# A first stage in which dense products, modulation products and the split of the operands are put in another order

## The reference

```python
m_l = (jax.nn.silu(c) @ mod_w + mod_b)[:, None, :]
m_c = jax.nn.silu(c_ctx) @ mod_w + mod_b
sh1_l, sc1_l, g1_l, sh2_l, sc2_l, g2_l = jnp.split(m_l, 6, axis=-1)
sh1_c, sc1_c, g1_c, sh2_c, sc2_c, g2_c = jnp.split(m_c, 6, axis=-1)
p_lat = _ada(x, norm1, sh1_l, sc1_l) @ w_in      # _ada = rmsnorm(x, g) * (1 + scale) + shift
p_ctx = _ada(ctx, norm1, sh1_c, sc1_c) @ w_in
```

## Time and profile before

| what | value |
| --- | --- |
| median of three runs | 2082.76 us (2080.64 to 2083.97) |
| the profiled execution, its own time | 2093.51 us |
| its span in the trace | 2091.7 us |
| TensorE, VectorE, ScalarE, GpSimd busy | 91%, 57%, 40%, 13% of the span |
| mean granted TensorE clock | 0.955 |
| the first stage in the trace | 0 to about 201 us |

### The profile page before, as it was taken

One profiled execution on the slowest core, in us unless ns is written; L12 is line 12 of the kernel. 1 busy time (PEld: TensorE's weight loads), 2 busy tenths in 40 slices (PEclk: granted clock), 3 DMA queues, 4 the chain that ended last, 5 costly groups with the idle time before them and its releaser, 6 DMA issues. The chain is left out here.

```text
span 2091.7 us, 42194 instructions
## 1 busy us (share of the span) xinstructions
PE 1906.8 (91%) x18192; PEld 1663.0 (80%) x18192; DVE 1189.3 (57%) x2005; ACT 834.7 (40%) x1533; POOL 282.0 (13%) x341
## 2 busy tenths in 40 slices
PE   5999787878788999999999889999979999979997
PEld 4787445877767888888987779999769999769997
DVE  3322756446455752353466767855667756657753
ACT  3321464314223421122243645544454445454432
POOL 0200300502304000001300420111021002121001
PEclk8999986997999999999999999999989999999998
DMA  7621872002033323323231055555325546325543
GB/s 249 165 81 61 275 229 81 4 19 87 5 120 104 96 86 101 96 86 101 90 121 52 1 182 162 182 184 183 98 81 162 191 154 199 101 81 162 182 161 101
DMA packets 249003, 255.04 MB, mean 122 GB/s; under 512 B 6914, under 2 KB 247186, under 8 KB 248690
## 3 DMA queue, kind: packets, MB, share of 16 engines
q1 hardware_dynamic: 247344, 251.19, 37.3%
q0 software_dynamic: 864, 0.98, 0.4%
q10 hardware_dynamic: 610, 0.18, 0.0%
HBM read 251.28 MB, written 1.05 MB: 121 GB/s over the span
## 5 line engine op out<-in xcount | busy, mean ns | idle before, releaser
L529 DVE TENSOR_TENSOR RING_rounded<-RING,SC_rounded 128x1024 fp32r<-128x1024 f32 (+2 forms) x390 | 459.3, 1221 | 253.3 <-ACT SC_rounded L522 253.2
L549 PE MATMUL bank<-OT_rounded,SC_rounded 128*128 128x256 f32 (+1 forms) x1808 | 578.2, 320 | 25.2 <-DVE RING_rounded L529 8.5
L550 PE MATMUL bank<-HT_rounded,SC_rounded 128*128 128x256 f32 (+1 forms) x1808 | 573.5, 317 | 0.0
L551 PE MATMUL bank<-OT_rounded,RING_rounded 128*128 128x256 f32 (+1 forms) x1808 | 571.0, 316 | 0.0
L522 ACT ACTIVATE SC_rounded<-RING 128x1024 fp32r<-128x1024 f32 (+2 forms) x390 | 372.2, 1006 | 330.5 <-DMA RING<-in_l_mlp_w 187.3
L549 PEld LDWEIGHTS bank<-OT_rounded,SC_rounded 128*128 128x128 f32 x1808 | 344.7, 191 | 57.3 <-DVE RING_rounded L529 10.3
L551 PEld LDWEIGHTS bank<-OT_rounded,RING_rounded 128*128 128x128 f32 x1808 | 344.2, 190 | 26.1
L550 PEld LDWEIGHTS bank<-HT_rounded,SC_rounded 128*128 128x128 f32 x1808 | 344.6, 191 | 22.6
L549 PE MATMUL bank<-PT_rounded,SC_rounded 128*128 128x256 f32 (+1 forms) x896 | 277.9, 310 | 4.7 <-DVE RING_rounded L529 4.7
L550 PE MATMUL bank<-PT_rounded,SC_rounded 128*128 128x256 f32 (+1 forms) x896 | 276.9, 309 | 0.0
L551 PE MATMUL bank<-PT_rounded,RING_rounded 128*128 128x256 f32 (+1 forms) x896 | 276.0, 308 | 0.0
(11 more groups left out here) (546 smaller groups left out, 2742.0 us busy)
## 6 DMA issues: line engine op xcount, KB each, us to landing
RING<-in_l_mlp_w SPq DMA_DIRECT2D x64, 1024.0 KB, 5.3
RING<-in_w_ffn_in SPq DMA_DIRECT2D x44, 1024.0 KB, 5.1
RING<-in_l_mod_w SPq DMA_DIRECT2D x40, 1024.0 KB, 6.2
RING<-in_l_w_in SPq DMA_DIRECT2D x25, 1024.0 KB, 5.5
RING<-in_w_ffn_out SPq DMA_DIRECT2D x16, 768.0 KB, 4.6
RING<-in_w_in SPq DMA_DIRECT2D x10, 1024.0 KB, 5.4
RING<-in_w_ffn_out SPq DMA_DIRECT2D x16, 640.0 KB, 4.1
PT<-in_l_mod_w SPq DMA_DIRECT2D x8, 1024.0 KB, 9.7
```

What stands on the lines that cost most here:

```text
L529: net.nc.vector.tensor_tensor(low, whole, net.high4(s, m)[:, 0:self.w.kts[s], :].bitcast(F32), ALU.subtract).then_inc(self.split_ready, 1)
L549: net.nc.tensor.matmul(bank[:, tokens], high, x_high, start=start, stop=False)
L550: net.nc.tensor.matmul(bank[:, tokens], high, x_low, start=False, stop=False)
L551: return net.nc.tensor.matmul(bank[:, tokens], low, x_high, start=False, stop=stop)
```

## The change

The order of all three compute engines in the first stage is rewritten, and nothing else. Parameter rows: `c` and `c_ctx` are still fetched by ScalarE, the 13 other early ones by SyncE, between the first modulation slab and the second. Front: the last token block is transposed in `turn_order` and each bank is announced by itself; VectorE copies five banks, ScalarE three; the inverse roots are spread before `add(0)`; VectorE multiplies two tiles, does the first pair, and the other six tiles after it. Sums of the slabs go to two buffers in turn (`mod_rows`), so `copy(k)` waits for `fold(k-2)` only. `products` takes one half m at a time, and adds and folds of the next pair are put between the dense products of the pair at hand. ScalarE rounds the first half of a weight slab ahead of a pair's shift (slab 0) or between two copies (slabs 1, 2); VectorE's `operand(p)` is cut into `shift(p)` and `split(p)`.

```diff
...
+    mod_rows = [mod.rows, net.SC[:, 8968:9224]]
...
-    copy_order = [6, 7, 0, 1, 2, 3, 4, 5]
+    turn_order, copies_by_dve, copies_by_act = [7, 6, 0, 3, 1, 4, 2, 5], [7, 6, 0, 1, 2], [3, 4, 5]
...
+        places = [(g, sum(c for _, c in tile[:n]), name, count)
+                  for g, tile in enumerate(ROWS) for n, (name, count) in enumerate(tile)]
+        n_now = len(ROWS[0])
...
+                if k == 0:
+                    fetch_rows(sp, places[2:n_now])
...
-                    last = nc.tensor.matmul(sections[:, 2 * k + m, :], mod.rows[:, P * m:P * m + P],
+                    last = nc.tensor.matmul(sections[:, 2 * k + m, :], mod_rows[k % 2][:, P * m:P * m + P],
...
-                for f in range(KT):
+                for f in turn_order if t == NCH - 1 else range(KT):
...
-                last.then_inc(turned, 1)
-            pe.wait_ge(c_ready, 2)
+                    if t == NCH - 1:
+                        last.then_inc(turned, 1)
             pe.wait_ge(copied, 2)
-            add(0)
...
             last.then_inc(root_spread, 1)
+            add(0)
+            pe.wait_ge(rows_in[0], 16 * (len(ROWS[0]) - 2))
+            pe.wait_ge(copied_by_act, len(copies_by_act))
+            turn_rows(0, net.ps[5])
             add(1)
-            pe.wait_ge(rows_in[0], 16 * (len(ROWS[0]) - 2))
-            pe.wait_ge(copied, KT)
-            turn_rows(0, net.ps[5])
             pe.wait_ge(rstd_ready, 1)
             fold(0)
             fold(1)
-            products(0, (0, 1))
+            pe.wait_ge(copied, len(copies_by_dve))
+            products(0, 0, (0, 1))
             add(2)
+            products(0, 1, (0,))
+            add(3)
             fold(2)
-            add(3)
+            products(0, 1, (1,))
             fold(3)
+            products(1, 0, (0, 1))
+            products(1, 1, (0, 1))
+            products(0, 0, (2, 3))
+            products(0, 1, (2, 3))
+            add(4)
+            products(1, 0, (2, 3))
+            add(5)
+            fold(4)
+            products(1, 1, (2,))
+            fold(5)
+            products(1, 1, (3,))
             pe.wait_ge(cols_ready, 1)
-            products(0, (2, 3))
-            products(1, (0, 1))
-            add(4)
-            products(1, (2,))
-            fold(4)
-            add(5)
-            products(1, (3,))
-            fold(5)
-            products(0, (4, 5))
-            products(1, (4, 5))
-            products(2, (0, 1))
+            for kts in ((0, 1), (2, 3)):
+                for m in range(2):
+                    products(2, m, kts)
+            products(0, 0, (4, 5))
             add(6)
-            products(2, (2,))
+            products(0, 1, (4,))
+            add(7)
             fold(6)
-            add(7)
-            products(2, (3,))
+            products(0, 1, (5,))
             fold(7)
-            products(2, (4, 5))
+            for q in (1, 2):
+                for m in range(2):
+                    products(q, m, (4, 5))
             for q in range(by_pairs):
-                products(q, (6, 7))
+                for m in range(2):
+                    products(q, m, (6, 7))
...
-                if k:
-                    act.wait_ge(mod.folded, k)
-                act.activation(mod.rows, mod.sums, ACT.Copy).then_inc(mod.copied, 1)
+                if k > 1:
+                    act.wait_ge(mod.folded, k - 1)
+                act.activation(mod_rows[k % 2], mod.sums, ACT.Copy).then_inc(mod.copied, 1)
...
-            fetch_rows(places[:n_now])
+            fetch_rows(act, places[:2])
...
-            copy(0)
+            for f in copies_by_act:
+                act.wait_ge(turned, turn_order.index(f) + 1)
+                act.activation(net.XT[:, f, :], net.ps[f][:, :], ACT.Copy).then_inc(copied_by_act, 1)
...
+            copy(0)
             copy(1)
+            part.high(act, 0, 0)
             operand(0)
-            highs(0)
+            part.high(act, 0, 1)
             copy(2)
+            part.high(act, 1, 0)
             copy(3)
+            part.high(act, 1, 1)
             operand(1)
-            highs(1)
             copy(4)
+            part.high(act, 2, 0)
             copy(5)
+            part.high(act, 2, 1)
             operand(2)
-            highs(2)
             copy(6)
             copy(7)
             operand(3)
             highs(3)
-            fetch_rows(places[n_now:])
+            fetch_rows(act, places[n_now:])
...
-            def operand(p):
...
+
+            def split(p):
                 for t in (2 * p, 2 * p + 1):
                     dve.wait_ge(high_ready, t + 1)
                     nc.vector.tensor_tensor(HR[:, t, :], HT[:, t, :], OR[:, t, :].bitcast(F32),
                                             ALU.subtract).then_inc(split_ready, 1)
...
-            dve.wait_ge(turned, NCH)
-            for f in copy_order:
+            def norm(t):
...
+            for f in copies_by_dve:
+                dve.wait_ge(turned, turn_order.index(f) + 1)
                 nc.vector.tensor_copy(net.XT[:, f, :], net.ps[f][:, :]).then_inc(copied, 1)
+            dve.wait_ge(rstd_ready, 1)
+            norm(0)
+            norm(1)
             take_rows(0, net.ps[5])
             dve.wait_ge(cols_ready, 1)
-            dve.wait_ge(copied, KT)
-            dve.wait_ge(rstd_ready, 1)
-            for t in range(KT):
-                nc.vector.tensor_tensor(HT[:, t, :], net.XT[:, t, :], rstd, ALU.mult).then_inc(normed, 1)
-            operand(0)
-            lows(0)
-            operand(1)
+            shift(0)
+            part.low(dve, 0, 0)
+            split(0)
+            part.low(dve, 0, 1)
+            for t in range(2, KT):
+                norm(t)
             lows(1)
-            operand(2)
+            shift(1)
+            split(1)
             lows(2)
-            operand(3)
+            shift(2)
+            split(2)
+            shift(3)
+            split(3)
             lows(3)
```

More of the change, by code:

```diff
@@ L2160, in first_stage, with fetch_rows @@
         part = Part(net, st, "in0", w_in, Operand(OR, HR), banks=6)
+        places = [(g, sum(c for _, c in tile[:n]), name, count)
+                  for g, tile in enumerate(ROWS) for n, (name, count) in enumerate(tile)]
+        n_now = len(ROWS[0])
+        def fetch_rows(queue, some):
+            for g, r, name, count in some:
+                a = ins[name]
+                if len(a.shape) == 2:
+                    a = a.rearrange("a b -> (a b)")
+                into = rows[r:r + count, g, :]
+                queue.dma_start(into, a.rearrange("(t p) -> t p", p=P)).then_inc(
+                    c_in if g == 0 and r < 16 else rows_in[min(g, 1)], 16)
         @st.sync
@@ L2232, in turn_rows, with products @@
                 nc.tensor.transpose(bank[:, 0:r], rows[0:r, g, :], ident[0:r, 0:r]).then_inc(rows_turned, 1)
-            def products(q, kts):
-                for m in range(2):
-                    if kts[0] == 0:
-                        part.ready(pe, q, m)
-                    for kt in kts:
-                        pe.wait_ge(split_ready, kt + 1)
-                        step = part.passes(q, m, kt, everything)
-                    if kts[-1] == KT - 1:
-                        step.then_inc(part.used, 1)
+            def products(q, m, kts):
+                if kts[0] == 0:
+                    part.ready(pe, q, m)
+                for kt in kts:
+                    pe.wait_ge(split_ready, kt + 1)
+                    step = part.passes(q, m, kt, everything)
+                if kts[-1] == KT - 1:
+                    step.then_inc(part.used, 1)
             pe.wait_ge(const_in, 16)
@@ L2341, in operand @@
                 act.activation(OR[:, t, :], HT[:, t, :], ACT.Copy).then_inc(high_ready, 1)
-            places = [(g, sum(c for _, c in tile[:n]), name, count)
-                      for g, tile in enumerate(ROWS) for n, (name, count) in enumerate(tile)]
-            n_now = len(ROWS[0])
-            fetch_rows(places[:n_now])
+            fetch_rows(act, places[:2])
             act.wait_ge(c_turned, 1)
@@ L2410, in modulate, with shift @@
                 dve.wait_ge(aff_ready, p + 1)
-            def operand(p):
+            def shift(p):
                 modulate(p)
```

17 lines of the change are left out of this document (7 added, 10 removed).

## The result

The changed kernel took 2069.35 us (median of 8 runs, 2067.62 to 2077.76), the kernel before 2085.14 in the same comparison (8 runs, 2080.64 to 2088.15): ratio 0.9926, 95% interval 0.9911 to 0.994. That is 15.8 us less; the forecast was 20.1. So it is faster, as forecast, by under 1%. The gain is some 4 us smaller than worked out. The time is 6.7 us above the 2062.7 worked out and 3.9 above 2065.5, the upper end of the forecast's own range; it lies 0.15 us inside the wide range, whose upper part stood for the rivals. Of the 6.7 us, 2.4 come from the kernel before, whose median is 2085.14 here and was 2082.76 in the three runs that the forecast started from; 4.3 are gain that didn't come.

The account below looks back on a forecast made before the run. Bound: TensorE's idle time and lower clock in the first stage, the second pair being the real bound. Stage end 200.78 to 180.7 (-20.1), taken off the median 2082.76, gives 2062.7 us; own range 2060 to 2065.5, wide range 2058 to 2069.5.

Parts of the forecast that it names:

- the wide range: Whole kernel time: 2058 to 2069.5 us, meant to hold the forecast and most of its rivals.
- The front: Start of first stage: earlier rows, copies and norms bring the first dense product to 21.8, 7.5 us earlier.
- The landings stay as they are; cost 0: DMA queue early in the first stage: rows on SyncE delay no slab, since the backlog covers them; cost 0.
- The second pair: Products of kt 2 and 3: the chain behind the second weight slab (27.45) sets their start at 33.85.
- The clock term: Three TensorE restarts in the first stage: 39 products at the lower clock lose 0.20 each, 7.9 us.
- The later stages: Behind the first stage: same code, starting on a barrier, so all of the 20.1 us gain should arrive.
- B: First stage: light products hold TensorE's clock down until after slab 3's fold; kt 2 at 35.2 to 38.0; chance 0.17.
- C: First stage: the clock stays low until the last fold; 4.7 us slower, 2087; chance 0.02.
- D: SyncE's queue: row issues held back like slab issues delay every landing; 2067, or 2107 at worst; chance 0.07.
- E: ScalarE's list: waiting for a weight slab ahead of a copy a fold needs costs 3 to 6 us; chance 0.12.
- the table load's move frees the SiLU wait: Start of first stage: with thirteen row issues off ScalarE, TensorE's 1.44 us wait for the SiLU goes.
- the six norms: VectorE in the front: six of eight norms leave the path to the first pair, worth 3.7 us.

Follow-up runs that it names:

- t1: The changed kernel as it is, timed a second time: 2070.65 us, ratio 0.992 [0.9903, 0.9936].
- p3: The changed kernel as it is, profiled a third time: 2071.81 us.
- t2: The changed kernel with the 13 parameter row fetches issued by GpSimd instead of SyncE, timed: 2070.91 us, ratio 0.9923 [0.9903, 0.9944].
- p4: The changed kernel with the 13 parameter row fetches issued by GpSimd instead of SyncE, profiled a third time: 2074.7 us.
- e3: The changed kernel with the third weight slab fetched ahead of the second modulation slab: 2073.96 us.
- p1: The kernel before, unchanged, profiled once more: 2076.46 us.
- p2: The kernel before, unchanged, profiled again: 2091.32 us.
- e4: The changed kernel with extra identity products, 8 ahead of the second add and 16 behind the second fold, to keep TensorE busy: 2072.39 us.
- e2: The changed kernel with all 15 early row fetches back on ScalarE, ahead of its table load: 2077.06 us.
- e5: The changed kernel with TensorE's list of products, adds and folds put back to the old order: 2085.03 us.
- e6: The kernel before with only TensorE's list of products, adds and folds in the new order: 2090.97 us.
- e7: The changed kernel with all eight VectorE norms ahead of the first pair, as before: 2071.82 us.
- t3: The kernel before with only the 13 row fetches moved to SyncE, timed: 2085.94 us, ratio 0.9993 [0.9975, 1.0012].
- e8: The kernel before with only the 13 row fetches moved to SyncE, single run: 2088.41 us.

## Why the prediction came out as it did

**Direction and mechanism right, two terms mis-sized.** The pairs' order and the end are what was worked out: the first dense product 6.3 us earlier (7.5 worked out), the restart at 59.18 gone, kt 2 released by VectorE's split of the activations behind the second weight slab. The chain behind that slab was worked out as 180.7 - 27.45 = 153.25; it measured 153.31 to 153.33 in five executions (t1, p3, t2, p4, e3), and up to 154.04 where the copy was late. The stretch from 35.30 to 69.92 was worked out as 34.4 and took 34.62. What failed are the landings, put at no cost, and the loss by the lower clock in the kernel before, put at 7.9.

**The front, 21.8 worked out, 23.00 measured.** The step that failed is "the queue never runs dry if the next issue is ahead of that. The landings stay as they are; cost 0". The second modulation slab was issued at 9.79, ahead of the first one's landing at 12.1 (3.08 + 9.0), so the condition was met; the rate fell all the same, to 315 GB/s from 11.0 to 14.5, as in every execution with the rows on SyncE. The second modulation slab came at 16.58 (15.4 worked out), the first weight slab's rounding started at 19.57 (18.4), the first product came 1.2 late. On average over all traces the rows on SyncE go with 0.6 us of this; the rest, and why, is open. The 27.45 that the sum started from was itself an early case (28.3 and 28.1 in p1 and p2). The chain between the slab and the product is right: 23.00 - 19.57 = 3.43, worked out 21.8 - 18.4 = 3.4. The row block on SyncE took until 9.79, against "at about 9.2 at the latest"; the prediction's bound of 0.43 for each issue was broken by the first one, 1.60 us.

**The second pair, 33.85 worked out, 35.30 measured.** 1.1 of it is the same landing (28.59 against 27.45). 0.3 is a step that I had as hidden, "as long as they cost under 0.7 more": the copy of the fourth slab's sums waited 0.29 for the fourth add, since the third add ran at the lower clock for 1.94 us, not 1.00. In t1 and t2 that wait isn't there. So the hiding was real and its margin smaller than I said. Behind it some 0.1 is added; the stage's end came 1.6 late, 182.29 against 180.7.

**The clock term, 7.9.** The other term that was mis-sized is "The lower clock costs 12+14+13 = 39 products at 0.20 = 7.9". It was read from one execution. The first restart's 12 products, 2.8 us at the full clock, take 5.25 us, 5.37 in p1 and 4.71 in p2: 2.5, 2.6 and 1.9 lost. Behind the second restart 2.8 are lost in the trace that was read, 1.5 less in p1 and 0.3 less in p2 (40.52 to 57.59 is 17.07). In the 5.7 us behind the third restart that one loses 13 x 0.20 = 2.6 us; in p1 18 products take 5.66 us, so 5.66 - 18 x 0.233 = 1.5 us are lost, and in p2 none. In sum 7.9, 5.4 and 4.5 us, on average 6.0. By the stage's end the kernel before is 200.78 where I read it and 198.9 on average over three. That 1.9 is all but this clock; in p2 a front that is 0.7 earlier and a wait before the fourth slab that is 1.0 longer (1.44 against 0.42) about cancel. The changed kernel is 182.29, 181.86 and 182.84, on average 182.3. The gain of the stage is therefore 16.6, not 18.5, and 1 - 16.6/2085.1 = 0.9920, beside the timed 0.9926 and 0.992. In sum: 20.1 worked out, 1.6 lost to landing and copy, 1.9 that the kernel before doesn't lose in its average execution.

**"The later stages ... all of it should arrive".** The time behind the stage (the span less the start of the next stage) is 1889.9, 1875.3 and 1890.9 in the kernel before and 1884.2, 1886.0 and 1886.2 in the changed one: means of 1885.4 and 1885.5. With a spread of 15.6 us in three executions of the kernel before, the means alone would not show that the gain arrives; the two timed ratios do, since 0.9920 from the stage lies within both intervals. The difference of 5.7 between the first two profiles, which is more than the prediction allowed for, is within that spread.

**Rivals.** B and C (light products hold the clock down) are refuted: the add at 28.80 takes 1.07, and 28.80 to 35.30 shows 1.00, with thin products among the dense ones since 25.83. That 35.30 touches B's 35.2 to 38.0 is chance: there TensorE's own work was to set kt 2, and here TensorE waits 0.84 us for VectorE. D (row issues on SyncE as slow as slab issues) is refuted at 13 in 6.2 us; in a small form it occurs, as the lower rate near 12 us. Its sign, a falling DMA share near 12, shows in p3 (0.75 from 12 to 13) and hardly in the changed kernel's execution (1.04). E (issue order) occurs in a small form too, the 0.29 us wait of the copy and the 1.97 us wait in e4. The forecast that the table load's move frees the SiLU wait holds (e2).

**Which part earns the gain.** Rows alone: ratio 0.9993 [0.9975, 1.0012]. TensorE's list alone: between 0.5 us lost and 1.4 gained. All but TensorE's list: 0.9973 [0.9961, 0.9986]. All: 0.9926. The parts bring more together than apart. My reading is that each removes one of several waits that end nearly together; the two traces of e5 and e6 show such waits, but no run takes them one by one. What I priced as a step of its own, the six norms (3.7 us), is worth 0.6 at the first product and 0 at the end (e7), because the first weight slab is as late.

## What to carry to other kernels

Before adding up the losses of a stage, find the transfer behind which its last chain starts: here the second weight slab, with 153.3 us behind it. What stands ahead of that landing, clock and norms included, is free until it passes it (e4, e7; in e2 it passed it), and the landing counts in full (3.04 us in e3). A low clock behind it is not free (0.4 us in e4). Read a term that comes from the clock or from a first transfer in several executions before it enters a sum: here one profile overstated the loss of the kernel before by 1.9 us in 200. An issue that comes ahead of the last landing need not keep the rate up (315 GB/s here, 349 before). And when an engine's list is reordered, reorder the lists that feed it in the same step; one alone moved idle time from place to place.

## What the runs showed of the hardware

The same idle time doesn't give the same clock. After 2.89 us of idle time at the same instruction TensorE restarted at 0.50 in the earlier trace rows and at the full clock in p2. In t3 its first product took 0.80 us, as in the earlier trace rows, and the clock was 0.51 over 5.72 us:

```profile
57.98 0.80 PE L549 MATMUL bank<-OT_rounded,SC_rounded 128*128 128x512 f32 x1 [2.89 <-DVE HT_rounded L2424]
```

In p1 and in e8 (the same kernel as t3) that product took 0.50 and the clock was 0.70 on average over the next 5.66 us: in p1 two products run at the full clock, and from 58.41 to 61.75 they run at the lower one. So the clock can also fall after the restart. A low stretch from a restart on lasted from 2.7 us (p1 from 41.97) to 6.11. After 3.49 us of idle time e5 began at the full clock too, and had 0.71 on average over the next 5.89 us.

An add (16 products of 32 columns, 1.07 us) took 1.94 at the lower clock, so such products follow the clock as dense ones do, and the clock rose while they stood among the dense ones (23.00 to 28.80).

The first transfers of the stage, from the same program, landed up to 1.0 us apart in two executions (second weight slab 28.55 in t1, 29.52 in p3), while the distance between the first two weight slabs kept to 0.02 us in six executions of the two versions (in e4 it was 1.2 us longer).

Thirteen small fetches (0.5 to 24 KB each) between two slabs of 1 MB in SyncE's queue went with 260 to 317 GB/s from 11.0 to 14.5 us in ten executions of ten; with these fetches on ScalarE or GpSimd it was 346 to 351 in eight of eight.
